# Output projections in three products of rounded parts, in a two-model transformer stack on one core

## What is computed

```python
for l in range(DEPTH):                      # block 1, DEPTH = 2
    h = rmsnorm(x, g_mix_pre[l])
    (...) = jnp.split(h @ w_in[l], SPLIT_POINTS, axis=-1)
    o_a = gated_deltanet(...)               # 512 channels
    o_b = dsa_attention(...)                # 256 channels
    o_c = hgrn2(...)                        # 256 channels
    mix = jnp.concatenate([o_a, o_b, o_c], axis=-1) @ w_out[l]     # output projection
    x = x + rmsnorm(mix, g_mix_post[l])
    h = rmsnorm(x, g_ffn_pre[l])
    x = x + rmsnorm(conv_geglu_ffn(h, ffn_w_up[l], ffn_conv[l], ffn_w_down[l]), g_ffn_post[l])
```

```python
    y = jnp.concatenate([_rms(y_lru), _rms(y_sb), _rms(y_fox)], axis=-1) * g_mix_out
    return y @ w_out                        # output projection, 1024 x 1024
```

## Time and profile before

| | us |
|---|---|
| Median of 3 runs | 3976.39 (3972.38 to 3984.34) |
| The profiled execution, its own time | 3969.55 |
| Its span in the trace | 3967.5 |
| TensorE busy | 3748.2 (94%) |
| DVE busy | 2190.1 (55%) |
| ACT busy | 1167.1 (29%) |
| POOL busy | 304.6 (8%) |
| Mean granted clock of TensorE | 0.972 |

### The profile page before, as it was taken

One profiled execution on the slowest core, in us unless ns is written; L12 is line 12 of the kernel. 1 busy time (PEld: TensorE's weight loads), 2 busy tenths in 40 slices (PEclk: granted clock), 3 DMA queues, 4 the chain that ended last, 5 costly groups with the idle time before them and its releaser, 6 DMA issues.

```text
span 3967.5 us, 48980 instructions
## 1 busy us (share of the span) xinstructions
PE 3748.2 (94%) x17670; PEld 2948.4 (74%) x17670; DVE 2190.1 (55%) x3553; ACT 1167.1 (29%) x1725; POOL 304.6 (8%) x503
## 2 busy tenths in 40 slices
PE   8988889998998889998999999999999999999999
PEld 6768558886778658886888775588878887656887
DVE  5866458845767547855554455455443335634332
ACT  3341333322431423322222234222222223422221
POOL 1200001100010001110110100011000001000000
PEclk9989799999998999999999999999999999999999
DMA  4300035543210025543554320355433333103323
GB/s 110 84 17 1 17 93 158 158 118 79 75 47 1 1 76 163 163 127 85 165 167 121 90 77 1 92 166 160 118 96 95 86 95 87 43 22 93 98 85 96
DMA packets 580045, 359.63 MB, mean 91 GB/s; under 512 B 20414, under 2 KB 559792, under 8 KB 579888
## 3 DMA queue, kind: packets, MB, share of 16 engines
q1 hardware_dynamic: 554480, 281.43, 25.5%
q0 software_dynamic: 25408, 76.11, 6.3%
HBM read 355.35 MB, written 2.10 MB: 90 GB/s over the span
## 4 chain that ended last, share of the span: by engine, by line
PE 83%; DVE 9%; ACT 3%; issue 3%; DMA 1%; DVEq 1%; ACTq 0%; POOL 0%; SPq 0%; POOLq 0%
PE ps L1304 16%; PE ps L1306 15%; PE ps L1305 15%; PE ps L1542 6%; PE ps L1546 6%; PE ps L1545 6%; PE ps L1355 5%; PE ps L1695 3%; DVE wl L2067 1%; PE ps L1458 1%; DMA wada<-in_w_ada 1%; PE ps L1438 1%; PE ps L1857 1%; PE ps L1416 1%; PE ps L1505 1%
## 5 line engine op out<-in xcount | busy, mean ns | idle before, releaser
L1304 PE MATMUL ps<-hh,wh 128*128 128x512 f32 x2912 | 1157.0, 397 | 46.9 <-DVE wl L2067 18.0
L1306 PE MATMUL ps<-hh,wl 128*128 128x512 f32 x2912 | 1140.8, 392 | 0.0
L1305 PE MATMUL ps<-hl,wh 128*128 128x512 f32 x2912 | 1140.7, 392 | 0.0
L2067 DVE TENSOR_TENSOR wl<-wring,wh 128x1024 fp32r<-128x1024 f32 x476 | 581.2, 1222 | 769.3 <-ACT wh L779 762.3
L779 ACT ACTIVATE wh<-wring 128x1024 fp32r<-128x1024 f32 x496 | 522.8, 1055 | 972.4 <-PE ps L1542 506.1
L1304 PEld LDWEIGHTS ps<-hh,wh 128*128 128x128 f32 x2912 | 551.4, 189 | 185.8 <-issue 50.2
L1306 PEld LDWEIGHTS ps<-hh,wl 128*128 128x128 f32 x2912 | 550.7, 189 | 116.9
L1305 PEld LDWEIGHTS ps<-hl,wh 128*128 128x128 f32 x2912 | 551.8, 189 | 112.4 <-issue 1.9
L1542 PE MATMUL ps<-ah,wh 128*128 128x512 f32 x1056 | 411.9, 390 | 1.9 <-DVE wl L2067 1.9
L1546 PE MATMUL ps<-ah,wl 128*128 128x512 f32 x1056 | 410.9, 389 | 0.0
L1545 PE MATMUL ps<-al,wh 128*128 128x512 f32 x1056 | 410.9, 389 | 0.0
(11 more groups left out here) (408 smaller groups left out, 3503.6 us busy)
## 6 DMA issues: line engine op xcount, KB each, us to landing
wring<-in_w_ffn_up SPq DMA_DIRECT2D x176, 512.0 KB, 4.9
wada<-in_w_ada POOLq DMA_DIRECT2D x384, 192.0 KB, 2.7
wring<-in_w_in SPq DMA_DIRECT2D x98, 512.0 KB, 5.0
wring<-in_ffn_w_up SPq DMA_DIRECT2D x88, 512.0 KB, 4.9
wring<-in_w_ffn_down SPq DMA_DIRECT2D x64, 512.0 KB, 3.9
wring<-in_w_out SPq DMA_DIRECT2D x32, 512.0 KB, 5.1
wring<-in_ffn_w_down SPq DMA_DIRECT2D x32, 512.0 KB, 4.0
wring<-in_w_ffn_down SPq DMA_DIRECT2D x16, 384.0 KB, 3.4
```

The lines of the kernel that those rows point to most:

```text
L1304: pe.matmul(dst, w, h, start=first, stop=False)
L1305: pe.matmul(dst, w, hlo, start=False, stop=False)
L1306: return pe.matmul(dst, wlo, h, start=False, stop=last)
L2067: v.tensor_tensor(wl[:, w, :, :], wring[:, p, h, :, :], wh[:, w, :, :].bitcast(F32), ALU.subtract)\
```

## The change

The output projections become tiles of the three-product kind.

- Activations: ACT rounds `oT` (or `o2`) slices 0 to 5 to `hh` while the mixer still runs (`high_part`, in steps 9 to 14 of block 1's loop, and in steps 7 to 10, 15 and 16 of block 2's attention), and POOL subtracts to get their low parts (`low_parts`, into `ol`, the memory of `oT` or `o2` itself). Slices 6 and 7 are rounded by ACT and subtracted by DVE at the end (`last_low_parts`), behind which `mix_ready` stands.
- Weights: every tile is split. The first two tiles' splits are moved ahead into the mixer (ACT after chunks 1 and 2 of the recurrence, or in steps 5 and 6 of the attention; POOL subtracts). The other six and the next FFN's first two are made by ACT ahead of its wait for the evicted tile, and by DVE right behind each eviction.
- TensorE takes slices 0 to 5 of two tiles first in both blocks, then 6 and 7 of both, then six whole tiles. In block 2, 15 products stand between the row sums and the cast.
- Some buffers move so that `wh` and `wl` are free there: `hS`, `ho`, and the evicted tiles of block 1 now go to `yT` instead of `hT`.

```diff
-POOL_SPLITS = 10
+POOL_SPLITS = 12
+        ol = [rounded("ol1", at[0], 8, T)]
         oT = take(8, T)
-        hS = take(NC, 2, 64)
-        ho = take(2, T)
+        hS = arena[:, at_bet:at_bet + 2 * T].rearrange("p (c q d) -> p c q d", c=NC, q=2)
+        ho = dnT[:, 9:11, :]
+        yT = dnT[:, 0:8, :]
...
+        ol.append(rounded("ol2", at[0], 8, T))
         o2 = take(8, T)
...
# POOL
+            def low_parts(o, lo):
+                for k in range(6):
+                    g.wait_ge(o_hi.sem, k + 1)
+                    g.tensor_tensor(lo[:, k, :], o[:, k, :], hh[:, k, :].bitcast(F32), ALU.subtract)\
+                        .then_inc(o_lo.sem, 1)
...
+                low_parts(oT, ol[0])
                 conditioning(ada[0], l * (ADA // 2))
...
                 g.wait_ge(small_loaded.sem, l * 208 + 208)
+                for n in range(2):
+                    g.wait_ge(w_hi.sem, DEPTH * TILES_1 + l * TILES_2 + 3 * NF + 21 + n)
+                    g.tensor_tensor(wl[:, n, :, :], wring[:, 0, n, :, :], wh[:, n, :, :].bitcast(F32), ALU.subtract)\
+                        .then_inc(wl_pool.sem, 1)
+                g.drain().then_inc(w_free[0].sem, 1)
+                low_parts(o2, ol[1])
...
# ACT
+            def high_part(o, k):
+                s.activation(hh[:, k, :], o[:, k, :], ACT.Copy).then_inc(o_hi.sem, 1)
...
+                    if c in (1, 2):
+                        s.wait_ge(dn_v.sem, dn_count("W", 3))
+                        split()
...
+                    if 9 <= t < 13:
+                        o_set.next(s)
+                        high_part(oT, t - 9)
+                    if t == 13:
+                        s.wait_ge(at_out.sem, 16)
+                    if 13 <= t < 15:
+                        high_part(oT, t - 9)
...
+                for k in (6, 7):
+                    o_set.next(s)
+                    high_part(oT, k)
                 s.preload_act_table_set("sqrt_and_others")
-                place[1] += OUT_SLOTS
-                mm_done.seen[id(s)][1] += KD
                 def y_square(k):
+                    split()
                     y_ready.next(s)
-                    if k >= KD - 2:
-                        split(after_out=True)
-                wide_norm([hT[:, k, :] for k in range(KD)], y_square, True)
+                wide_norm([yT[:, k, :] for k in range(KD)], y_square, True)
...
+                    if 5 <= i < 7:
+                        split()
+                    if 7 <= i < 11 or 15 <= i < 17:
+                        k = i - 7 if i < 11 else i - 11
+                        o_set.next(s)
+                        high_part(o2, k)
...
# TensorE
+            def first_out(lo, half, ks):
+                if ks[0] == 0:
+                    first[half] = parts_ready(True), bank()
+                w, b = first[half]
+                for k in ks:
+                    m = product(ps[:, b, :], wh[:, w, k, :], hh[:, k, :], wl[:, w, k, :], lo[:, k, :],
+                                k == 0, k == KD - 1)
+                if ks[-1] == KD - 1:
+                    m.then_inc(mm_done.sem, 1)
+            def rest_out(lo):
+                mix_ready.next(pe)
+                for half in range(2):
+                    first_out(lo, half, (6, 7))
+                for n in range(2, KD):
+                    tile(lo=lo)
+                place[1] += OUT_SLOTS
...
                 sums(0)
-                first_out(0, range(3))
+                pe.wait_ge(o_lo.sem, 6)
+                first_out(ol[0], 0, range(3))
                 sums(1)
-                first_out(0, range(3, 6))
+                first_out(ol[0], 0, range(3, 6))
                 pe.wait_ge(rec_done.sem, n_norm[0])
                 cast(0)
                 cast(1)
-                first_out(1, range(6))
-                mix_ready.next(pe)
-                for half in range(2):
-                    first_out(half, (6, 7)).then_inc(mm_done.sem, 1)
-                pe.drain().then_inc(w_free[p].sem, 1)
-                for n in range(3):
-                    out_pair(oT)
+                first_out(ol[0], 1, range(6))
+                rest_out(ol[0])
...
-                row_sums(4, 2)
+                pe.wait_ge(o_set.sem, 6)
+                row_part(4, 0, 2)
+                row_part(4, 1, 2)
+                pe.wait_ge(o_lo.sem, 6)
+                first_out(ol[1], 0, range(5))
                 row_cast(4)
-                mix_ready.next(pe)
-                for n in range(4):
-                    out_pair(o2)
+                first_out(ol[1], 0, range(5, 6))
+                first_out(ol[1], 1, range(6))
+                rest_out(ol[1])
...
# DVE
+            def last_low_parts(o, lo):
+                for k in (6, 7):
+                    v.wait_ge(o_hi.sem, k + 1)
+                    v.tensor_tensor(lo[:, k, :], o[:, k, :], hh[:, k, :].bitcast(F32), ALU.subtract)
+                v.drain().then_inc(mix_ready.sem, 1)
...
-                v.drain().then_inc(mix_ready.sem, 1)
+                last_low_parts(oT, ol[0])
                 for k in range(KD):
                     if k >= 2:
                         sum_add(k - 1)
                     b = filled()
-                    v.tensor_copy(hT[:, k, :], ps[:, b, :])
+                    v.tensor_copy(yT[:, k, :], ps[:, b, :])
                     free()
                     v.sem_inc(y_ready.sem, 1)
-                post_norm(lambda k: par[:, 0, A_G + 8 + k:A_G + 9 + k], 2)
+                    split()
+                post_norm(yT, lambda k: par[:, 0, A_G + 8 + k:A_G + 9 + k])
...
                     v.sem_inc(x_ready.sem, 1)
-                mod_norm(2, 2)
+                    split()
+                mod_norm(2)
```

More of the change, by code:

```diff
@@ L443, in program @@
         mix_ready = ev("mix_ready")
-        mix_early = ev("mix_early")
+        o_set = ev("o_set")
+        o_hi = ev("o_hi")
+        o_lo = ev("o_lo")
         c_act = ev("c_act")
@@ L764, in begin, with split @@
                 n_split[0] = 0
-            def split(i=None, whole=False, first=None, after_out=False):
+            def split(i=None, whole=False, first=None):
                 p, half = place[1] % 2, place[2]
@@ L1347, in turn_raw @@
                 m.then_inc(v_turn.sem, 1)
-            def out_pair(src):
-                p = loaded()
-                for half in range(2):
-                    b = bank()
-                    for k in range(KD):
-                        m = pe.matmul(ps[:, b, :], wring[:, p, half, k, :], src[:, k, :],
-                                      start=k == 0, stop=k == KD - 1)
-                    m.then_inc(mm_done.sem, 1)
-                pe.drain().then_inc(w_free[p].sem, 1)
             def norm_part(k, n, lhsT=None):
@@ L1850, in cast @@
                     i.then_inc(bc_done.sem, 1)
-                p = loaded()
-                banks = [bank(), bank()]
-                def first_out(half, ks):
-                    for k in ks:
-                        i = pe.matmul(ps[:, banks[half], :], wring[:, p, half, k, :], oT[:, k, :],
-                                      start=k == 0, stop=k == KD - 1)
-                    return i
                 sums(0)
-                first_out(0, range(3))
+                pe.wait_ge(o_lo.sem, 6)
+                first_out(ol[0], 0, range(3))
                 sums(1)
                 n_norm[0] += 1
-                first_out(0, range(3, 6))
+                first_out(ol[0], 0, range(3, 6))
                 pe.wait_ge(rec_done.sem, n_norm[0])
@@ L2997, in _ @@
                 for j in (6, 7):
-                    factor(j, o2[:, j, :])
-                v.drain().then_inc(mix_ready.sem, 1)
+                    factor(j, o2[:, j, :]).then_inc(o_set.sem, 1)
+                last_low_parts(o2, ol[1])
+                w_hi.seen[id(v)][1] += 2
+                n_split[0] += 2
+                half[0] = 1 - half[0]
                 n_sq[0] += 12
```

54 lines of the change are left out of this document (22 added, 32 removed).

## The result

Four runs of the changed kernel have a median of 3917.62 us (3911.39 to 3923.97); the kernel before, run beside it, has 3974.39 us (3966.6 to 3984.34). The ratio is 0.9856, 95% interval 0.9824 to 0.9888. The forecast was 3925.5, from 3908 to 3948. The profiled execution took 3923.97 us, its span 3922.2, against a forecast of 3918.7 for it. The changed kernel's runs lie at two levels, two at 3911.4 and two at 3923.9 with mean granted clocks of TensorE of 0.975 to 0.976 and 0.971; the profile is of the upper one.

The account below looks back on a forecast made before the run. TensorE, busy 94% of the span, was taken as the bound. Block 1's -24.5 and block 2's -26.4 us sum to -50.9, taking the median from 3976.39 to 3925.5 us, range 3908 to 3948.

Parts of the forecast that it names:

- Price of a tile: Output projections: a tile falls from 7.12 to 5.42 us, worth 1.7 us each, eight tiles a projection.
- block 1's and block 2's projection: The output projections themselves: gains of 12.3 and 12.6 us in block 1's layers, 14.4 us in each of block 2's.
- What would show it: Signs expected in the new profile: 192 triples more per projection, products 0.23 us apart, one stop of about 1.2 us.
- Last low parts hidden: Block 1's projection: low parts of inputs 6 and 7, 3.8 us behind the casts, hidden under 18 products of 4.1 us.
- The wait ahead of the third tile: With only two part buffers, TensorE stands 1.2 us there, once in each projection.
- the second rival: Projections: splits keep up only partly, all six later tiles wait 1.2 us more, +28.8, total 3954.3; chance 0.06.
- the fourth: Projections: parts of the first tiles come late, TensorE waits some 10 us a projection, total 3965; chance 0.04.
- The tail: Behind each projection: last tile's end to DVE's first scaling falls from 7.3 to 5.5 us, gain 1.8, four times.
- ScalarE ahead of the projection: ACT's added early roundings and splits cost 1.2 us in block 1's loop and 1.5 in block 2's attention.
- Whether POOL slows DVE: POOL's added work in the mixer stages, charged 0.8 us in block 1 and 1.5 in block 2; bounds 0 and 12.0.
- a rival at 0.15: Mixer stages: POOL and DVE shut each other out, about half of 48 us on the path, total 3944.9; chance 0.15.
- The rival of 4100 us: Projections: all 192 products run at the lower clock, 43.6 us each projection, +174 in all; chance 0.04.

Follow-up runs that it names:

- Block 1 alone: Three products of rounded parts only in block 1's output projections, block 2 as before the change, against the changed kernel: 3945.45 us, ratio 0.9923 to the kernel before.
- the halves: Changed kernel with the third tile of each output projection split in two halves, each with its own handover: 3918.04 us.
- undoing the order: Changed kernel with VectorE's subtractions for the feed-forward network's first two tiles again between its reciprocal and first scaling: 3923.45 us.
- the settings: Changed kernel with GpSimd's subtractions replaced by setting the buffers to zero: one execution, 3912.34 us.
- a wait did not help: Kernel of moved parts (early roundings behind block 1's loop, weight splits ahead of block 2's logits) plus a TensorE wait ahead of block 1's outputs: 3935.8 us.

## Why the prediction came out as it did

The forecast of the total was 8 us high for the median and 5 us low for the profiled execution. Most of its terms held.

- **Price of a tile, block 1's and block 2's projection.** 16.0 us less in each layer of block 2 (forecast 16.2). In block 1 16.1 and 10.7 against 14.1 and 14.4; the split between the layers is the clock's. Like beside like, the two projections behind outputs at the full clock differ by 14.2 us (72.25 and 58.07), the two behind outputs at the lower one by 12.6 (74.21 and 61.59). Tiles stand 5.57 us apart for the 5.42 of the forecast. Block 1 alone confirmed that the sums add. Under "What would show it", the count of 192 triples is a slip: a projection has 192 such products, 64 triples.
- **Last low parts hidden.** Right, with no stop behind 18 products.
- **The wait ahead of the third tile.** 1.07 to 1.11 us (forecast 1.2), once in a projection, shown by the halves. No later tile waits, so the second rival is out. So is the fourth: GpSimd's subtractions were all done before the sums (0.00 us busy in the projection windows), and TensorE had no stop at its first products.
- **The tail.** 5.4 us for 5.5; 1.1 of it shown by undoing the order.
- **ScalarE ahead of the projection.** 1.1 us in the loop for 1.2. In block 2 about 0.8 (38.9 to 38.06, an upper bound, since the settings still hold VectorE up) for 1.5.
- **Whether POOL slows DVE: the mis-sized term.** I charged 0.8 and 1.5 us a layer from a row in which it did not, and put the lock on a rival at 0.15. It acts: 1.1 to 1.6 us in the loop and 3.3 in the attention, some 9 us in all for 4.6 charged, but far from the rival's 24. A part of these 9 us is the clock, lower in layer 1's loop and for 3.4 us of each attention. The rival priced GpSimd's busy time; what counts is which VectorE instructions start under it. In the attention eight scalings of both layers grew by 9.0 us together, while copies from PSUM, other instructions with an input in PSUM and reciprocals of one column beside the same subtractions kept their times.

  The prediction also says that no row of the trace before shows such a pair. That was a misreading. Timeline of the kernel before, in the search for the top keys, beside one of GpSimd's early splits:
```profile
154.10 2.40 POOL L711 TENSOR_TENSOR wl<-wring,wh 128x1024 fp32r<-128x1024 f32 x1 [4.17 <-ACT wh L779]
...
155.21 0.41 DVE L2433 MATCH_REPLACE8 arena<-arena 128x256 f32<-128x256 f32 x1
155.65 1.00 DVE L2435 TENSOR_SCALAR arena<-arena 128x256 f32<-128x256 f32 x1
```
  The search's own instructions go on undisturbed, but its one TENSOR_SCALAR of 256 columns takes 1.00 us and ends at 156.65, just behind GpSimd's 156.50; the shortest of that line takes 0.36. I took GpSimd's even durations as evidence against a lock, and it is the later of the two that is held up: the place to look was VectorE's durations under GpSimd's, and by this row each scaling in the attention had a wait of up to 2.4 us to fear.

  The Trainium skill, page "SBUF — State Buffer", section "Who interferes with whom", says that the loser of the shared ports is blocked for the whole instruction and that tensor_scalar can enter a two-port mode; the 2.38 us that end with GpSimd's subtraction agree. It also says that two SBUF inputs collide only with a GpSimd that reads: the product at 1.48 beside subtractions and 0.42 beside settings agrees. The prediction gave the page's rule as if GpSimd had to read in both cases; the page asks that only for two SBUF inputs, and the scaling at 0.95 us beside a setting, which reads nothing, agrees with the page.
- **The clock.** No term of the sum had it beyond the first products, and it moves single runs by more than any other error: the 12.4 us between the two levels of the changed kernel are more than the 5 to 8 us by which the forecast was off. The rival of 4100 us did not occur: the products themselves ran at 1.00 from the second sums on. What stays open is why block 1's outputs fall to the lower level. In the 14 profiles, cut as in the table, they did so in 6 of 9 layers with a loop of 46.5 us or less, in 2 of 3 at 47.4 to 47.6, and in 3 of 16 at 48.6 or more. In all 11 they began at the full clock, which fell 1.1 to 2.9 us later and stayed low for 20 to 27 us with TensorE busy throughout the outputs. The loop's length alone doesn't decide: behind 49.17 us the outputs took 11.75 (VectorE's two subtractions back, layer 1) and behind 49.20 us 17.75 (the changed kernel, layer 1). A link with it is possible; its cause is not settled, and a wait did not help. Each such layer costs 9.5 us (17.75 for 11.75, 61.59 for 58.07). That is near the 12.4 us between the changed kernel's two levels, but only the upper one has a profile, so this is not shown. Nor are the outputs the only place: the kernel with settings reaches its first loop at 399.54 us, at a granted clock of 0.94, the changed kernel at 392.43, at 0.96, with the same work up to there.

## What to carry to other kernels

Work put on GpSimd is not free because GpSimd is idle: look at which VectorE instructions start while it runs, and whether they touch SBUF alone with two inputs or as a tensor_scalar (a single stretched one in the trace before tells it); give such work to a stretch in which VectorE waits, or to VectorE itself. Price a change stage by stage and check it stage by stage, each with its granted clock: at the same clock a stage repeats within 0.1 us (the attention of the changed kernel took 42.16, 42.18, 42.15 and 42.18 in its two profiles, all at 0.96, but the same code took 43.36 at 0.92), while totals move by 12 us. And a lower clock in another stage can hide what an edit saved (here 9.5 of 11.2 us), so an improvement of a few us needs its stages and its total.

## What the hardware did that was not expected

- A GpSimd instruction that reads nothing, a setting of 128x1024 values (0.96 us), holds up VectorE's TENSOR_SCALAR from 0.35 to 0.95 us.
- The same 96 records of block 1's outputs take 11.75 us at a granted clock of 1.00 and up to 18.95 at 0.53, with TensorE busy all the time in either case. Where they were slow, the clock was full when they began and fell 1.1 to 2.9 us into them.
